# VectorE's order around the first expert products: roots, gate rows and second routing rearranged in a decoder step with PEER experts

## What is computed

```python
q = (xt @ w_query).reshape(blk, PEER_HEADS, PEER_KEY_DIM)        # 8 heads, 256
s1 = jnp.einsum('nhd,hkd->nhk', q[..., :128], k1)                # 128 keys a side
s2 = jnp.einsum('nhd,hkd->nhk', q[..., 128:], k2)
sc1, i1 = lax.top_k(s1, 16); sc2, i2 = lax.top_k(s2, 16)
cand = (sc1[..., :, None] + sc2[..., None, :]).reshape(blk, 8, 256)
top_sc, top_c = lax.top_k(cand, 16)
experts = e1 * 128 + e2                                          # of 16384
gate = jax.nn.softmax(top_sc, axis=-1)
act = gelu(einsum('nd,nhkd->nhk', xt, u_tab[experts]))
out = einsum('nhk,nhkd->nd', gate * act, v_tab[experts])
```

## Time and profile before

| | |
|---|---|
| median of three runs | 1625.16 us |
| profiled execution, its span | 1822.2 us |
| bytes moved by DMA | 643.92 MB |
| of that on GpSimd's queue (the gathers) | 570.49 MB |
| TensorE busy | 1105.9 us (61%) |
| VectorE busy | 1060.3 us (58%) |
| ScalarE busy | 273.3 us (15%) |
| GpSimd busy | 1088.7 us (60%) |

### The profile page before, as it was taken

The page is one execution under the profiler, slowest core; times in us unless marked ns, Lnnn a source line. Parts: engine busy times, 40 slices in busy tenths (PEclk is TensorE's granted clock), DMA queues, the critical chain, the costliest instruction groups (busy, mean ns, idle before and its releaser), DMA issues.

```text
span 1822.2 us, 16621 instructions
## 1 busy us (share of the span) xinstructions
PE 1105.9 (61%) x5557; PEld 544.7 (30%) x5557; DVE 1060.3 (58%) x2708; ACT 273.3 (15%) x660; POOL 1088.7 (60%) x1194
## 2 busy tenths in 40 slices
PE   9766999987787789963433367543433344343345
PEld 8764444445665575540000011100000000000011
DVE  5454776737575484876677848764647444444420
ACT  3332144303210242210000000000000000000000
POOL 5523355655536555667666666666666766666664
PEclk9887998999878899996565578755565566665657
DMA  7777698999998999999999899999999999999997
GB/s 244 270 256 286 246 345 327 381 363 354 389 336 321 373 370 386 407 414 385 366 364 363 343 360 385 355 372 375 370 370 388 382 365 367 384 365 371 372 371 295
DMA packets 178652, 643.92 MB, mean 353 GB/s; under 512 B 21728, under 2 KB 21736, under 8 KB 178440
## 3 DMA queue, kind: packets, MB, share of 16 engines
q0 software_dynamic: 156672, 570.49, 80.8%
q1 hardware_dynamic: 21320, 70.28, 10.7%
q10 hardware_dynamic: 576, 2.10, 0.3%
HBM read 637.24 MB, written 5.16 MB: 353 GB/s over the span
## 4 chain that ended last, share of the span: by engine, by line
PE 31%; DVE 22%; POOL 17%; another core or an unknown queue 14%; issue 13%; ACT 2%; DMA 1%; ACTq 0%; DVEq 0%; POOLq 0%
PE pp L754 14%; POOL ring L714 8%; DVE ring L1229 6%; PE y L1046 4%; PE pp L764 4%; POOL w_ring L714 3%; PE pp L835 2%; POOL C_sample L714 2%; POOL act_T L714 2%; DVE w_ring L1229 2%; DVE act_T L1229 1%; DVE C_sample L1229 1%; POOL keys_T L714 1%; DVE lists L1558 1%
## 5 line engine op out<-in xcount | busy, mean ns | idle before, releaser
L714 POOL DMA_INDIRECT ring<-in_u_experts,expert_idx x316 | 302.0, 956 | 296.9 <-issue 79.3
L714 POOL DMA_INDIRECT ring<-in_v_experts,expert_idx_by_token x342 | 328.2, 960 | 224.3 <-issue 90.0
L1229 DVE SCALAR_TENSOR_TENSOR ring<-ring,x_normed 128x1024 f32<-128x1024 f32 x316 | 372.2, 1214 | 112.5 <-DMA ring<-in_u_experts,expert_idx 76.1
L1046 PE MATMUL a<-ring,z_columns 128*32 128x512 f32 x660 | 213.8, 957 | 184.3 <-DMA ring<-in_v_experts,expert_idx_by_token 110.7
L754 PE MATMUL pp<-act_T,w_ring 128*128 128x128 f32 (+2 forms) x1280 | 288.6, 387 | 13.2 <-ACT act_T L1889 5.7
L1046 PE MATMUL y<-ring,z_columns 128*32 128x512 f32 x792 | 226.6, 763 | 85.2 <-DMA ring<-in_v_experts,expert_idx_by_token 51.2
L754 PEld LDWEIGHTS pp<-act_T,w_ring 128*128 128x128 f32 x1280 | 198.4, 202 | 104.3 <-issue 96.7
L1046 PE MATMUL a<-w_ring,z_columns 128*32 128x512 f32 x124 | 79.3, 956 | 74.3 <-issue 35.9
L764 PE MATMUL pp<-w_ring,act_T 128*128 128x128 f32 (+1 forms) x832 | 108.2, 289 | 20.4 <-issue 9.4
L1046 PEld LDWEIGHTS a<-ring,z_columns 128*32 128x32 f32 x660 | 37.5, 146 | 275.7 <-issue 274.6
L764 PEld LDWEIGHTS pp<-w_ring,act_T 128*128 128x128 f32 (+1 forms) x832 | 100.7, 184 | 34.0 <-issue 31.4
(11 more groups left out here) (354 smaller groups left out, 1820.7 us busy)
## 6 DMA issues: line engine op xcount, KB each, us to landing
w_ring<-in_w_all SPq DMA_DIRECT2D x104, 512.0 KB
ring<-in_v_experts,expert_idx_by_token POOLq DMA_INDIRECT x342
ring<-in_u_experts,expert_idx POOLq DMA_INDIRECT x316
ring<-in_w_all SPq DMA_DIRECT2D x8, 512.0 KB, 9.1
x_res<-in_x_prompt SPq DMA_DIRECT2D x4, 512.0 KB, 7.2
C_sample<-in_state_C SPq DMA_DIRECT2D x4, 512.0 KB
out_C_s<-C_sample ACTq DMA_DIRECT2D x4, 512.0 KB
out_y_p<-x_res SPq DMA_DIRECT2D x16, 128.0 KB
```

Of the source, the lines that this page charges most:

```text
L714: pool.indirect_dma_start(out=slot[s], out_offset=None, in_=a["u_experts"] if kind == "u" else a["v_experts"], in_offset=bass.IndirectOffs ...
L1046: ins = pe.matmul(total[low:low + 32, half * 512:(half + 1) * 512], zcols[:, part % 2, lo:lo + 32], rhs, start=False, stop=True, skip_grou ...
L1229: dve.scalar_tensor_tensor(out=slot[s], in0=slot[s], scalar=1.0, in1=xn_now[:, :], op0=ALU.mult, op1=ALU.mult, accum_out=dots[:, part % 4, ...
```

## The change

Only the lists of counts are changed; no instruction is added or removed. VectorE's steps:

```diff
-DVE_STEPS = ("r8 d21 r5 d15 g1 d12 r1 d4 r1 ...
+DVE_STEPS = ("r8 d6 r1 d3 r1 d3 r1 d3 r1 d3 r1 d18 g1 d12 r1 d4 r1 ...
```

How many steps are taken by which point (only these differ in the three lists):

```diff
-DVE_BY  77: 8   78: 29   79: 54   80: 54   81: 55   82: 70
+DVE_BY  77: 14  78: 47   79: 54   80: 62   81: 63   82: 70
-PE_BY   85-90: 0        91: 1  93: 2  95: 3  96: 4  98: 5  100: 6  102: 7  104: 8
+PE_BY   85-87: 1  88: 2  91: 3  93: 4  95: 4  96: 5  98: 6  100: 7  102: 8  104: 8
-ACT_BY  79-84: 0   85: 1
+ACT_BY  79-84: 1   85: 1
```

More of the change, by code:

```diff
@@ L211 @@
          "sample": (1, slice(MAX_P, MAX_W), [(6, ALL)])}
-DVE_STEPS = ("r8 d21 r5 d15 g1 d12 r1 d4 r1 d1 r1 d3 r1 d2 r1 d2 r1 d4 r1 d2 g1 d2 r1 d4 r2 d24 g1 d24 r1 d2 r1 d1 "
+DVE_STEPS = ("r8 d6 r1 d3 r1 d3 r1 d3 r1 d3 r1 d18 g1 d12 r1 d4 r1 d1 r1 d3 r1 d2 r1 d2 r1 d4 r1 d2 g1 d2 r1 d4 r2 d24 g1 d24 r1 d2 r1 d1 "
              "r1 d1 r1 d3 r1 d1 g1 r5 d34 g1 d19 r1 d3 r1 d1 r2 d1 r1 d6 r1 g1 d4 r2 d3 r1 d1 r1 d1 f1 d7 r1 d4 r2 "
```

## The result

The changed kernel takes 1647.61 us (median of four, 1645.07 to 1650.33), the kernel before 1625.43 us beside it: a ratio of 1.0142, 95% interval 1.013 to 1.0155. It is slower by some 23 us. Forecast were 1619 us, 1603 to 1632.

What follows compares the result with a forecast made beforehand. Gathers were taken to set the pace from 800 us, TensorE's path to decide from 183 to 345 us: 7 us relief less 1 for v groups gives 6, so 1625.16 becomes 1619 us, range 1603 to 1632.

Steps and rivals of the forecast that it cites:

- The hole is not on TensorE's path: From 183.36 to 345 us TensorE was said never to wait for a gathered row, a weight or a VectorE product.
- the points tie the gathers: GpSimd may send a row only when a VectorE product or TensorE v group, at fixed places between projections, frees its slot.
- the hole: 166 to 201 us, only 79 GB/s moved while GpSimd waits for expert numbers: 28.3 us of lost transfer time.
- (a): VectorE, six products ahead of the roots: they fill a 6.85 us wait; roots end about 134.5 instead of 133 us, free.
- (b): VectorE's second routing with twelve products between: done at 164.0 instead of 200.9 us; new stop of some 15 us until v5.
- (c): VectorE's gate rows and u gate: reached at 182.4 us, ready 184.7, free either way; list step ahead of memset hidden by 10 us.
- (d): ScalarE's first expert gate behind the gate rows: product 31 due at 180.1 us, 5 us of slack, costs nothing.
- Rival (3): Slower: another ScalarE stall in 166 to 205 us, or its product 31 wait outlasting 10 us of cover; 1631 or 1637 us; 19%.
- (e): TensorE's v groups one or two ahead: moved, not added; the last row may land late, cost taken as 0 to 1 us.
- the relief of 6.1 us: First part of the gain on TensorE's path from 183 to 345 us, beside 7.0 us of issue gaps; bounds 0 and 13.1 us.
- rival (2): Nothing is kept: early rows only leave room later, and ScalarE's 12.75 us stand belongs to its program place; 1625 us; 24%.
- third convolution earlier than 336.45 us: Sign of being right: TensorE's third convolution starts 4 to 13 us earlier, the rest of the trace shifted by that alone.

Runs made afterwards that it cites:

- e6: The changed kernel with ScalarE's first expert gate behind chunk 3 and TensorE's v groups at the points of the kernel before: 1621.78 us, ratio 0.9983.
- e4: The kernel before with only the six products moved ahead of the roots: 1624.09 us, ratio 1.0000.
- e7: The changed kernel with TensorE's v groups back at the points of the kernel before, ScalarE's gate still ahead of chunk 0: 1635.57 us, ratio 1.0067.
- e1_before: The kernel before, unchanged, run and profiled once more: 1623.27 us, ratio 0.9994.
- e5: The changed kernel with ScalarE's gate behind chunk 3 and the first v group behind chunk 4, later v groups at their new points: 1640.27 us, ratio 1.0099.
- e9: As e6, but the first four v groups on TensorE one point earlier than before: 1620.86 us, ratio 0.9982.
- e12: The kernel before with input chunks 3 and 5 summed over half of the input, 5.7 us of TensorE's work left out: 1621.55 us, ratio 0.9986.
- e8: As e6, but the list step and products 40 to 47 behind the memset again: 1624.44 us, ratio 1.0001.
- e10: As e6, but ScalarE's gate behind its read of chunk 0: 1627.23 us, ratio 1.0021.

## Why the prediction was wrong

**What bounds the stretch.** "The hole is not on TensorE's path" and "the points tie the gathers" were right, and they are why closing the hole brings little (2.8 us in e6). What I did not draw from it is the other half: if slots come free only by TensorE's and VectorE's points, TensorE's chain from 150 to 320 us sets the time, and no edit may add to it. I priced delays there as covered.

**(a) and (b), VectorE.** The mechanism came as described: expert numbers at 160.4 us (forecast 164.0), the long wait for them gone, a new stop before v5. That stop was put at 197 to 212 us; it is 11.49 us until 201.12 us. By themselves the six products are worth 0.0 us (e4). GpSimd gets a few waits of 2.4 to 3.1 us on products that now stand behind routing steps. The hole was mis-sized: 9.4 us of transfers, not 28.3.

**(c)** VectorE reaches the gate rows at 178.99 us (forecast 182.4), without a wait. But they are ready at 157.8, not at 184.7 us, so VectorE is 21 us late at them; that this costs nothing is the prediction's second branch ("free either way"), since the logarithms run at 226.98 us behind chunk 7 without a wait. The list step ahead of the memset costs nothing with the gate in time (e6). Right in the outcome.

**(d), the first step that failed.** The rule written there was right: what exceeds the slack and one chunk of 5.6 us stops TensorE. Its input was wrong. I set product 31 at 180.1 us against chunk 0's read at 189.4. Product 31 came at 176.8 us, but chunk 0 is finished at about 162 and wants reading then, because the gate rows are ready at 158 us. The rule with these numbers: the read is 178.4 - 162.1 = 16.3 us late, less 5.6 us, 10.7 us; measured 11.07. With the slower chunk behind it (8.31 us at a granted clock of 0.50) this is 13.7 us (e7 against e6), put at nothing. The 25.6 us that VectorE stood at the gate rows are 4.56 in e1_before: the gate rows come 26 us earlier here, the last product ahead of them only 5 (it ends at 154.0 instead of 159.1 us). The gap between two engines, which is all that a slack is, was the number least to be trusted. Rival (3) named this mechanism ("if ScalarE's wait for product 31 outlasts its 10 us of cover"), priced it by another row at 6 us and gave it 19%.

**(e), the second.** The v groups ahead of before were put at 0 to 1 us, with 6.4 us from issue to use of a row. That figure came from one row, the third behind a stop. In the changed kernel it is 7.8 us (v3 leaves at 182.49, the group starts at 190.26 us; v7, also the third row behind a stop, takes as long, 203.60 to 211.43 us), in e5 12 us. The longer time is the usual one. In the page of e1_before these lines end in the median from issue to landing; in the page that the prediction was read from there is none for the gathers:

```profile
w_ring<-in_w_all SPq DMA_DIRECT2D x104, 512.0 KB, 6.6
ring<-in_v_experts,expert_idx_by_token POOLq DMA_INDIRECT x342, 11.9
ring<-in_u_experts,expert_idx POOLq DMA_INDIRECT x316, 11.4
```

The due times were wrong too, as in (d): TensorE asks for v group 0 at 189.05 us, and in e5 at 185.5 us, not at 200, because its chunks start at 156 instead of 183 us, while v3 leaves only 3 to 5 us earlier than the 187 forecast. In e5 4.6 of the 10.36 us would have been left even with the 6.4 us. In the changed kernel the waits are 10.9 us, the two slow groups 3.3 more, and against e7 the v groups' points cost 23.1 - 10.9 = 12.2 us. It also feeds itself: TensorE waits for v rows, the chunks that VectorE's `gated` needs are late, no products are made, GpSimd stops 17.1 us, and the next v rows are late in turn.

**The sum.** No run shows the relief of 6.1 us: it was TensorE's 2.85 us behind ScalarE's stand of 12.75 us, and the 14.45 - 11.25 = 3.2 us that two chunks took too long. In e1_before there is no such stand: in 140 to 350 us no wait of ScalarE ends with "remote", and TensorE's nine chunks run without a gap, 5.62 us each. So it is not shown either that the stand belongs to a place in the program, as rival (2) has it: e1_before is the same program. The 197 us between span and median was carried over as a constant; it should have been a reason to doubt every due time. For the same reason the sign "third convolution earlier than 336.45 us" says nothing: it comes at 318.62 us, and that is 30 us later than in e1_before. Two signs of being wrong did come: TensorE idle ahead of v groups, and ScalarE standing over 8 us (10.12 us until 198.01 us).

**Weights beside the gathers.** No kernel here shows a TensorE wait for a weight between 140 and 350 us, though 342 to 418 GB/s were moved in the stages of 150 to 350 us of the changed kernel and of e1_before. In the page of e1_before a weight load of 512 KB lands 6.6 us after its issue, a gather of as much 11.4 to 11.9 us.

**Open.** Why a chain 5 us shorter gives back only 2 to 3 us. The traces of e6, e9 and e12 lose 2.5 to 3.9 us of transfers more than e1_before in 450 to 600 us, but e4 loses 3.2 more there without being slower, and e1_before loses the least of all thirteen traces there (3.2 us; ten lose 5.7 to 7.1, fast and slow kernels alike), so this is no proof. Which part of e8's edit undoes e6's gain. And what the hole is worth with no stop behind it: every kernel here with VectorE's new order has one, the shortest of 8.79 us (e9).

## What to carry to other kernels

The profile here that was longer than the timed runs, with waits that no row explains, had the durations right (a chunk 5.62 us in both) but not the slack: the distance between two engines' times is what it got wrong. When a profile is like that, profile again, or count every slack in it as unknown. Before an engine that empties another's output banks is given a step with a wait of its own, set the earliest time that the step can be reached against the time at which what it waits for is done, and subtract the banks; e10, e7 and the changed kernel all follow that subtraction. And where freed slots drive the transfers near their highest rate (419 GB/s in e5, 184 to 196 us), a consumer taken earlier has to be set against the landing time measured at that rate (12 us there, a median of 11.4 to 11.9 us in e1_before, not the 6.4 us of one row), and a hole in the transfers is not worth its bytes if the slots behind it still wait for the same engine: here the version with VectorE's order, the gate behind chunk 3 and the v groups where they were is the one that beats both (e6, 1621.78 us).

## What the hardware showed that I had not expected

A row of 128 x 4 KB that left GpSimd at 183.68 us was not used until 195.83 us by an engine that waited for it, while 419 to 420 GB/s were moved: 12 us, twice the 6.4 us read before, and close to the median of all gathers in e1_before (11.4 to 11.9 us). And the idle time of 11.07 us on TensorE cost more than itself: the first chunk behind it took 8.31 instead of 5.62 us, with a granted clock of 0.50 in 180 to 184 us; behind 6.17 us in e10 the clock is 0.50 from 176 to 182 us, and six chunks take 35.44 instead of 33.7 us.
